# Twelve sums of squares over heads in the first block: two float32r matmuls instead of one native fp32 matmul

## The reference

```python
def rms_norm(x, g):
    xf = x.astype(jnp.float32)
    y = xf * lax.rsqrt(jnp.mean(xf * xf, axis=-1, keepdims=True) + EPS)
    return (y * g.astype(jnp.float32)).astype(x.dtype)
# hgrn2_branch, four heads of 128:
    o = rms_norm(o, norm_g).reshape(B, S, HG_HEADS * HG_DV)
# stick_breaking_branch, eight heads of 64 for q and for k:
    qh = rms_norm(q.reshape(B, S, SB_HEADS, SB_DH), qn_g).transpose(0, 2, 1, 3)
    kh = rms_norm(k.reshape(B, S, SB_HEADS, SB_DH), kn_g).transpose(0, 2, 1, 3)
```

## Time and profile before

| | |
|---|---|
| median of three runs | 3385.81 us (3385.58 to 3386.06) |
| span of the profiled execution, first to last instruction | 3384.0 us |
| mean granted TensorE clock | 0.999 |
| busy share PE / weight load / DVE / ACT / POOL | 100% / 81% / 50% / 39% / 54% |
| the same from 150 to 350 us: PE, DVE, ACT | 100%, 74%, 58% |

### The profile page before, as it was taken

One profiled execution on the slowest core, in us unless ns is written; L12 is line 12 of the kernel. 1 busy time (PEld: TensorE's weight loads), 2 busy tenths in 40 slices (PEclk: granted clock), 3 DMA queues, 4 the chain that ended last, 5 costly groups with the idle time before them and its releaser, 6 DMA issues.

```text
span 3384.0 us, 46786 instructions
## 1 busy us (share of the span) xinstructions
PE 3367.8 (100%) x15450; PEld 2747.3 (81%) x15450; DVE 1701.2 (50%) x2655; ACT 1318.5 (39%) x1819; POOL 1811.5 (54%) x2325
## 2 busy tenths in 40 slices
PE   9999999999999999999999999999999999999999
PEld 5888777888888887888888888888887888888887
DVE  8887785544553438614434434544358334243444
ACT  4365664222232226735633222322237545532222
POOL 5444445655555556553455555555556543465554
PEclk9999999999999999999999999999999999999999
DMA  5212552322222223331222222222223222222223
GB/s 225 84 66 69 175 168 100 113 93 99 93 100 93 99 95 104 100 124 64 69 100 101 99 93 99 93 100 94 99 93 117 89 100 75 81 95 98 99 93 118
DMA packets 94603, 344.34 MB, mean 102 GB/s; under 512 B 10625, under 2 KB 11009, under 8 KB 94098
## 3 DMA queue, kind: packets, MB, share of 16 engines
q1 hardware_dynamic: 87410, 313.69, 27.2%
q10 hardware_dynamic: 7072, 29.02, 2.7%
HBM read 336.34 MB, written 2.13 MB: 100 GB/s over the span
## 4 chain that ended last, share of the span: by engine, by line
PE 81%; issue 10%; POOL 7%; ACT 0%; DVE 0%; DMA 0%; DVEq 0%; POOLq 0%; ACTq 0%
PE ps L486 25%; PE ps L488 25%; PE ps L487 25%; POOL w_lo L477 7%; PE ps L964 1%; PE ps L946 1%; PE ps L652 1%; PE ps L654 1%; PE ps L653 1%; PE ps L955 0%; PE ps L928 0%; PE ps L618 0%; PE ps L619 0%; POOL xres L455 0%; DMA arena<-arena 0%
## 5 line engine op out<-in xcount | busy, mean ns | idle before, releaser
L477 POOL TENSOR_TENSOR w_lo<-raw,w_hi 128x256 fp32r<-128x256 f32 x2268 | 1789.4, 821 | 1553.9 <-ACT w_hi L1050 1553.8
L1050 ACT ACTIVATE w_hi<-raw 128x1024 fp32r<-128x1024 f32 x568 | 598.8, 1057 | 1024.4 <-PE ps L488 1006.7
L486 PE MATMUL ps<-a_hi,w_lo 128*128 128x512 f32 x2208 | 873.6, 396 | 0.3 <-DVE a_lo L1779 0.3
L488 PE MATMUL ps<-a_hi,w_hi 128*128 128x512 f32 x2208 | 861.1, 390 | 0.0
L487 PE MATMUL ps<-a_lo,w_hi 128*128 128x512 f32 x2208 | 860.0, 390 | 0.0
L486 PE MATMUL ps<-b_hi,w_lo 128*128 128x512 f32 x2128 | 830.1, 390 | 4.5 <-DVE b_lo L1851 4.0
L487 PE MATMUL ps<-b_lo,w_hi 128*128 128x512 f32 x2128 | 828.6, 389 | 0.0
L488 PE MATMUL ps<-b_hi,w_hi 128*128 128x512 f32 x2128 | 828.6, 389 | 0.0
L486 PEld LDWEIGHTS ps<-a_hi,w_lo 128*128 128x128 f32 x2208 | 414.7, 188 | 99.1 <-issue 15.2
L488 PEld LDWEIGHTS ps<-a_hi,w_hi 128*128 128x128 f32 x2208 | 414.4, 188 | 87.9
L487 PEld LDWEIGHTS ps<-a_lo,w_hi 128*128 128x128 f32 x2208 | 414.9, 188 | 83.3 <-issue 0.5
(11 more groups left out here) (278 smaller groups left out, 2769.3 us busy)
## 6 DMA issues: line engine op xcount, KB each, us to landing
raw<-in_stream SPq DMA_DIRECT2D x570, 512.0 KB, 3.2
arena<-in_mod_w ACTq DMA_DIRECT2D x32, 512.0 KB, 4.1
arena<-in_mod_w SPq DMA_DIRECT2D x16, 512.0 KB, 11.4
arena<-arena ACTq DMA_DIRECT2D x16, 256.0 KB, 3.7
arena<-cum_rows ACTq DMA_DIRECT2D x2, 2048.0 KB, 9.4
xres<-in_x_t SPq DMA_DIRECT2D x4, 512.0 KB, 5.4
arena<-in_first SPq DMA_DIRECT2D x8, 256.0 KB, 11.7
xres<-in_x_t ACTq DMA_DIRECT2D x1, 2048.0 KB, 8.2
```

The costliest lines, as they stand in the source:

```text
L477: last = pool.tensor_tensor(w_lo[:, s, part], raw[:, s, part], w_hi[:, s, part].bitcast(F32), ALU.subtract)
L486: pe.matmul(out, lo, x_hi, start=start, stop=False)
L488: return pe.matmul(out, hi, x_hi, start=False, stop=stop)
L1050: act.activation(w_hi[:, slot, :], raw[:, slot, :], ACT.Copy).then_inc(hi_ready, 1)
```

## The change

Each of the twelve statistics is now made from two float32r matmuls on `sq_split`. ACT squares the tile twice, once in fp32 into the old buffer and once rounded into `sq_hi` (`head_square`), and the second raises `square_full`. DVE subtracts the one from the other into `sq_lo` (`head_split`) and raises `square_split`, for which PE now waits (`head_stats`). There is one pair `sq_hi`, `sq_lo`, so ACT waits for all earlier statistics. The block-diagonal ones are rounded once into `pair_sum`; for the HGRN norm the weights are minus ones (a column of `neg_tri`), and ACT takes the sign out. The placement of `head_split` in DVE's order is written out by hand.

```diff
+            def head_stats(weights):
+
+                need(pe, rt_ready, c.rt.at(0))
+                need(pe, aux_evacuated, c.aux.at(0))
+                pe.wait_ge(square_split, c.split.at(1))
+                pe.matmul(ps[:, 7, :], weights, sq_lo, start=True, stop=False)
+                pe.matmul(ps[:, 7, :], weights, sq_hi, start=False, stop=True).then_inc(stat_done, 1)
...
-            def stats_level(h, n, weights=ones_p):
-                stats(1, weights)
+            def stats_level(h, n):
+                head_stats(pairs)
                 hgrn_level(h, n)
...
             def norm_level(h):
-                stats(1)
+                head_stats(minus_ones)
...
+            def head_square(tile):
+
+                need(act, stat_done, c.sq.at(0))
+                act.activation(spare_square(c.sq.n), tile, ACT.Square)
+                act.activation(sq_hi, tile, ACT.Square).then_inc(square_full, 1)
...
             def sb_operand(dst):
                 evacuate(dst, ACT.Copy)
                 act.drain()
-                square(dst)
+                head_square(dst)
...
+            def head_split():
+
+                dve.wait_ge(square_full, c.split.at(1))
+                c.split.n += 1
+                dve.tensor_tensor(sq_lo, spare_square(c.sq.n), sq_hi.bitcast(F32), ALU.subtract).then_inc(square_split, 1)
...
-                def levels(self, first, end):
+                def levels(self, first, end, beside=lambda: None):
                     for n in range(first, end):
                         self.decayed(n)
                         if n + 2 < len(LEVELS):
                             self.exponents(n + 2)
+                        beside()
                         self.merge(n)
...
-                head.levels(7, 8)
+                head.levels(7, 8, lambda: None if head.h else head_split())
...
+            dve.tensor_copy(pair_sum[:, :], pair_ones[:, :])
...
-            heads[0].levels(3, 7)
+            heads[0].levels(3, 5)
+            heads[0].levels(5, 6, head_split)
+            heads[0].levels(6, 7)
...
             for h in range(1, HG_HEADS):
                 heads[h].levels(0, 2)
+                head_split()
                 gated_conv(h - 1)
                 pass_a(4)
-                heads[h].levels(2, 5)
+                heads[h].levels(2, 3)
+                heads[h].levels(3, 4, head_split)
+                heads[h].levels(4, 5)
...
-                heads[h].levels(6, 7)
+                heads[h].levels(6, 7, head_split)
...
             pass_a(2)
+            head_split()
             hgrn_norm(HG_HEADS - 1)
```

More of the change, by code:

```diff
@@ L210, in build @@
         pair_ones = sb("pair_ones", [P, P])
+        pair_sum = sb("pair_sum", [P, P], F32R)
         neg_tri = sb("neg_tri", [P, P], F32R)
@@ L595, in stats @@
                 c.rt.n += 1
+            def head_stats(weights):
[5 more added lines that the diff above has]
+                c.split.n += 1
+                c.sq.n += 1
+                c.rt.n += 1
             def x_stats():
@@ L756, in beside_values @@
                     stats(CT)
-            def stats_level(h, n, weights=ones_p):
-                stats(1, weights)
+            minus_ones, pairs = neg_tri[:, 0:1].to_broadcast([P, P]), pair_sum[:, :]
+            def stats_level(h, n):
+                head_stats(pairs)
                 hgrn_level(h, n)
@@ L775, in _ @@
             hgrn_level(0, 5)
-            project(bank_a(), lambda: stats_level(0, 6, pair_ones[:, :]))
+            project(bank_a(), lambda: stats_level(0, 6))
             hgrn_level(0, 7)
-            project(bank_a(), lambda: stats_level(0, 8, pair_ones[:, :]))
+            project(bank_a(), lambda: stats_level(0, 8))
             hgrn_level(0, 9)
@@ L785, in _ @@
                 hgrn_level(h, 3)
-                project(bank_a(), lambda: stats_level(h, 4, pair_ones[:, :]))
+                project(bank_a(), lambda: stats_level(h, 4))
                 hgrn_level(h, 5)
-                project(bank_a(), lambda: stats_level(h, 6, pair_ones[:, :]))
+                project(bank_a(), lambda: stats_level(h, 6))
                 hgrn_level(h, 7)
@@ L792, in _ @@
             project_half(0, lambda m: hgrn_out(HG_HEADS - 1) if m == 0 else None)
-            values_2(lambda t: stats(1) if t == 0 else None)
+            values_2(lambda t: head_stats(minus_ones) if t == 0 else None)
             c.op.n += 1
@@ L1285, in _ @@
                 act.wait_ge(head_done, h)
-                square(ps[:, 6, :])
+                head_square(ps[:, 6, :])
                 hgrn_decays(2)
@@ L1289, in _ @@
                 hgrn_decays(3)
-                inverse_rms(P)
+                inverse_rms(P, sign=-1.0)
                 hgrn_decays(4)
@@ L2089, in _ @@
             heads[0].merge(2)
-            heads[0].levels(3, 7)
+            c.sq.n += CT
+            heads[0].levels(3, 5)
+            heads[0].levels(5, 6, head_split)
+            heads[0].levels(6, 7)
             end(heads[0], heads[1], conv_low)
@@ L2204, in add_raw @@
                 split_sum()
-            c.sq.n += 3 * HG_HEADS + CT + 2
+            c.sq.n += 2
             add_tiles([(m, modp[:, 2 * KT + m:2 * KT + m + 1]) for m in range(KT)], True)
```

## The result

The changed kernel takes **3404.26 us** (median of 4 runs, 3403.65 to 3406.14), the kernel before 3385.69 us (4 runs, 3385.32 to 3386.06). The ratio is 1.0056 [1.0044, 1.0067], 18.6 us slower. The profiled execution has a span of 3401.9 us, 17.9 us over the one before, and a mean granted clock of 0.996.

The account below looks back on a forecast made before the run. PE, busy for 100% of the span, was taken as the bound. Saving, q of head 0, stalls and clock: -4.7 + 0.6 + 17.3 + 4.2 = +17.4 us, giving 3403.2 us, 0.5% slower; range 3396.0 to 3408.0 us.

Parts of the forecast that it names:

- The main term: k of heads 1 to 3: DVE's split stands behind four products, so PE stalls three times 5.75 us, 17.3 us.
- The saving of 0.39 us a statistic: On PE, two float32r passes replace a native fp32 matmul at twelve statistics: 4.7 us less.
- q of head 0: PE waits there for a split that is a little late: 0.6 us.
- Eight splits at nothing: Splits for q of heads 1 to 3, four norms and k of head 0 are in time: no cost.
- The clock: PE's clock falls behind each of the three long stalls, at 1.4 us a fall: 4.2 us more.
- if the slow part lasts twice as long, 8.4: Upper bound of the clock's cost behind the three stalls, 8.4 us; the lower bound was 0.
- the forecast by itself: Stalls of 5.3 to 6.0 us at k of heads 1 to 3, three clock falls: 3401.5 to 3404 us, 58%.
- The clock did not stay up: Rival: the three stalls come, but PE runs at full clock behind all or most: 3399.0 us, 19%.
- The shorter stalls: Rival: DVE's chain before the k split runs with POOL idle, stalls of 3.4 us each: 3391.9 us, 8%.
- The covered splits: Rival: DVE reaches the k split before PE needs it, leaving only the 4.7 us saving: 3381.1 us, 5%.
- The dearer case: Rival: slow clock lasts longer, or one of eight tight splits is late by 0.5 us each: 3404 to 3412 us, 10%.

## Why the prediction was right

**The main term held in mechanism, place and size.** The trace shows three waits for the split where they were predicted: at 236.4, 282.9 and 330.3 us (said: near 237, 283 and 328). Three times 5.75 = 17.3 us was predicted, 5.28 + 5.28 + 5.62 = 16.2 measured. In head 1, with the 0.60 us added by which this execution's times are early, the split ended at 236.85, where 236.90 was said. It got there by two errors that cancel: it started at 235.64 instead of 235.83 and took 1.21 us instead of 1.07. ACT's later hand-over freed the first two products from POOL (0.42 us each), DVE's wait for the second square in the q split took the same time back, and the prediction had let these two cancel. What was off is PE's arrival, 231.12 + 0.60 = 231.72 instead of 231.3: PE had lost 0.5 us at 203.70 (below), and what it loses ahead of a wait for DVE comes off that wait. This is the 0.5 us by which the term was too large in head 1; for heads 2 and 3 it was not worked out. That the order is the cause, and not the added work, was read from the rows of before and is shown by the two half-edits: moving either side alone removes 10.7 and 16.4 us.

**The saving of 0.39 us a statistic** held: in the version with both orders moved the pair of head 1 takes 0.47 us to the next start at full clock, as in the second block. A pair that has waited takes 0.54, by its slower first matmul.

**q of head 0**: 0.6 predicted, 0.47 measured, with the split as what ended it.

**Eight splits at nothing**: right. Four waits are all that stands at L603. Two small slips stand in the working and no term of the sum hangs on them: by its own terms PE is early at q of head 1 by three savings less the 0.6 us, 0.6 us and not 0.9, and the slowest products and split of the rows make a stall of about 6.0 us, not 6.2.

**The clock** was mis-sized. The step "3 x 1.4 = 4.2 us" took one fall of 3.4 us as the measure. The wait filled with matmuls puts it at 5.3 us by the runs, 5.7 in the stretch. The records tell why: at 282.9 and 330.4 us PE worked for 4.4 and 4.8 us at 0.50, where 578.60 had 3.4 us with PE idle for part of it; the granted clock was low for 3.4 us in head 1 and for 6.8 in heads 2 and 3. The fall came 4.8, 2.7 and 3.4 us after PE had begun to idle, so in head 1 PE worked through 3.1 us of the slow part, and in the other two through the last 4.4 and 4.8 us. The end "if the slow part lasts twice as long, 8.4" had named this and was not taken.

The Trainium skill, "TensorE: Matmul & The Clock Gate", section "Why this matters for your kernels", warns of long idle gaps. In the changed kernel the trace agrees, at all three waits of 5.1 to 5.5 us. The half-edit on DVE shows that waits of 2.19 and 2.53 us can do it too.

**Not in the sum**: 0.5 us at 203.70, a wait of 0.4 and a slower first matmul of 0.1, for an operand's remainder. Before, DVE made the four remainders of that piece from 199.16 in 3.59 us and was 1.4 us early; now, with 0.60 added, it starts 0.66 us later and takes 4.42 us, with POOL at work beside it from 198.92 instead of 200.01. The second term is the old fall of the clock, which the changed kernel has at 594.49 for 6.8 us instead of 3.4 at 578.60, for 0.4 us. The 1.1 us too much at the waits and the 1.1 to 1.9 us too little at the clock, with these two, leave the sum 1.1 us below the median: **it was better than its terms**, since their errors had opposite signs. That part was luck: the median lies in the stated range, but just above the 3401.5 to 3404 us that the forecast by itself gave.

The rivals fell as follows. The clock did not stay up. The shorter stalls would have needed all four products fast; two were. The covered splits came in no version with DVE's order as the change has it. The dearer case came in its first half, the longer slow clock, at the very lower end of its range, 3404 us, and had been given 10%.

What stays open: why the waits in heads 1 and 2 are alike and that in head 3 is 0.3 us longer, whether the number of falls is what parts the runs of the half-edit on DVE, and why the low clock near 580 us lasts longer in all versions but the one with native k, whether that hangs on when PE comes there. That was not tried.

## What to carry to other kernels

When a faster instruction needs one more operand from another engine, look for the place of its producer in that engine's order first, and price the distance between the two places: here 4.7 us of saved matmuls stood against 16 us of waiting for a subtraction of a microsecond. Both sides can be moved. Moving the consumer alone left waits of 1.5 to 1.8 us and no fall of the clock; moving both to level 8, where head 0 has them, left two waits of 0.2 us. And once the large wait is gone, an engine that saves a few tenths finds the next producer that was only just in time, so of 4.7 us saved 2.7 arrive.

## What the runs showed of the hardware

- **The clock falls behind waits shorter than the shortest one of before that did it.** 3.96 us was the row of before; 2.19 us did it at 276 us and did not at 233 us, 2.53 us did at 320; waits of 1.50 to 1.83 us did not in three places. These are places in one trace each; the kernel with the waits of 2.19 and 2.53 us has runs over 5 us apart. In the changed kernel the three falls cost 5.3 us. Every fall that was read lasted 3.3 to 3.4 us or 6.8 us.
- **DVE's subtraction with two inputs in SBUF** takes 0.69 us while POOL is idle (at 221.75 in the changed kernel) and 1.21 while it works (at 235.04), the 256-column products 0.42 and up to 0.96, but the merge that reads PSUM 0.73 in either case (at 230.36 us after the change with POOL idle, at 236.72 in the version with only PE's order moved with POOL at work). The Trainium skill, "GPSIMD Engine Reference", in the table of its section "Specifications", has GpSimd's SBUF interfaces shared with VectorE, with contention where an instruction has two SBUF inputs. The trace agrees. POOL's instruction beside the slow ones:

```profile
233.08 3.75 POOL L478 TENSOR_TENSOR w_lo<-raw,w_hi 128x256 fp32r<-128x256 f32 x4 [6.97 <-ACT w_hi L1064]
```

- **PE's first matmul behind a wait** takes 0.30 to 0.34 us to the next start at full clock, where 0.23 is usual (0.30 at 184.97, 0.34 at 203.70 in the changed kernel). A short wait costs this 0.1 us on top of its length.
- A second square on ACT of 0.62 us delays work far behind it although ACT is busy for only 58% of the stretch: DVE waits for it, and what DVE then hands back to ACT is late. In the kernel with native k, PE waited 0.41 us for the very square that had been in time.
